# One decoder step on one core: sample bias table, page indices and first weight loads moved to the first two stages, and sample scores on column halves

## The reference

```
mod = silu(c) @ w_ada + b_ada                       # shift, scale, gate, twice
h = x * (1 + sc1) + sh1
mix = mixer(h @ w_in)                               # attention
x = layer_norm(ALPHA * x + (1 + g1) * (mix @ w_o))
h = x * (1 + sc2) + sh2
x = layer_norm(ALPHA * x + (1 + g2) * hier_moe(h))  # 16 experts, 2 per token
```

## Time and profile before

| | us |
|---|---|
| median of 3 runs | 3181.93 (3181.4 to 3189.69) |
| profiled execution, own time | 3175.63 |
| its span, first to last instruction | 3174.2 |
| PE busy in the span | 2614.7 (82%) |
| DVE, ACT, POOL busy | 651.6, 507.9, 443.4 |
| mean granted TensorE clock | 0.90 |

### The profile page before, as it was taken

One profiled execution on the slowest core, in us unless ns is written; L12 is line 12 of the kernel. 1 busy time (PEld: TensorE's weight loads), 2 busy tenths in 40 slices (PEclk: granted clock), 3 DMA queues, 4 the chain that ended last, 5 costly groups with the idle time before them and its releaser, 6 DMA issues. The chain is left out here.

```text
span 3174.2 us, 39101 instructions
## 1 busy us (share of the span) xinstructions
PE 2614.7 (82%) x15984; PEld 1359.7 (43%) x15984; DVE 651.6 (21%) x1761; ACT 507.9 (16%) x1222; POOL 443.4 (14%) x670
## 2 busy tenths in 40 slices
PE   5699999999999945666768637998999599999970
PEld 2244444444444523454545434554445244444430
DVE  0100000000000001122223245773243211111108
ACT  1000000000000002222322325662000011111111
POOL 1000100000001112323110113551000100100110
PEclk9799999999999957788878868999999699999995
DMA  7765847749558324635378424456555389988735
GB/s 316 284 221 204 320 184 261 274 150 345 213 212 310 126 81 188 240 135 225 121 224 308 150 72 148 145 189 215 182 203 177 143 312 338 367 311 276 266 113 185
DMA packets 222305, 693.11 MB, mean 218 GB/s; under 512 B 27360, under 2 KB 41920, under 8 KB 194763
## 3 DMA queue, kind: packets, MB, share of 16 engines
q1 hardware_dynamic: 180212, 478.77, 42.4%
q0 software_dynamic: 38896, 201.85, 17.3%
q10 hardware_dynamic: 3024, 9.96, 0.8%
HBM read 664.01 MB, written 166.88 MB: 262 GB/s over the span
## 5 line engine op out<-in xcount | busy, mean ns | idle before, releaser
L426 PE MATMUL bank<-ring,xt 128*128 128x512 f32 (+1 forms) x2048 | 852.2, 577 | 19.7 <-PEq L436 11.6
L426 PEld LDWEIGHTS bank<-ring,xt 128*128 128x128 f32 x2048 | 378.7, 191 | 484.0 <-issue 472.2
L2812 PE MATMUL bank<-ring,hsT 128*128 128x512 f32 x768 | 339.7, 596 | 0.8 <-DVE hsT L2871 0.8
L2130 PE MATMUL bank<-ring,xt 128*128 128x512 f32 x512 | 224.8, 599 | 8.4 <-DMA ring<-in_w_o 8.4
L2812 PEld LDWEIGHTS bank<-ring,hsT 128*128 128x128 f32 x768 | 144.9, 191 | 174.8 <-issue 173.6
L460 DVE TENSOR_TENSOR mod<-bank,mod 128x512 f32 x4 | 2.8, 691 | 970.7 <-PE bank L215 970.7
L452 ACT ACTIVATE proj_stage<-bank 128x512 f32<-128x512 f32 (+2 forms) x80 | 41.1, 514 | 958.9 <-PE bank L426 938.7
L2831 PE MATMUL bank<-wd,hidT 128*128 128x512 f32 x384 | 171.2, 599 | 11.4 <-ACT hidT L2858 11.4
L2130 PEld LDWEIGHTS bank<-ring,xt 128*128 128x128 f32 x512 | 97.5, 192 | 128.6 <-issue 128.6
L472 POOL DMA_DIRECT2D proj<-proj_stage x64 | 35.3, 551 | 825.9 <-ACT proj_stage L452 825.9
L215 PE MATMUL bank<-ring,ct 128*32 128x512 f32 x768 | 106.5, 694 | 33.6 <-DMA ring<-in_w_ada 33.2
(11 more groups left out here) (466 smaller groups left out, 2613.3 us busy)
## 6 DMA issues: line engine op xcount, KB each, us to landing
ring<-in_w_ada SPq DMA_DIRECT2D x48, 2048.0 KB, 16.3
ring<-in_w_gate_up SPq DMA_DIRECT2D x48, 2048.0 KB, 9.8
ring<-in_w_in SPq DMA_DIRECT2D x30, 2048.0 KB, 9.1
out<-in_cache_dil POOLq DMA_DIRECT2D x7, 8176.0 KB, 41.9
wd<-in_w_down SPq DMA_DIRECT2D x24, 2048.0 KB, 9.4
ring<-in_w_o SPq DMA_DIRECT2D x16, 2048.0 KB, 9.6
ring<-in_cache_dil SPq DMA_DIRECT2D x16, 1024.0 KB, 13.9
rows<-in_cache_dil SPq DMA_DIRECT2D x16, 1024.0 KB, 11.6
```

What stands on the lines that cost most here:

```text
L426: mm = pe.matmul(R.banks[t][0:n, 0:width], R.xt[:, 8 * s + k, t0:t0 + n], R.ring[:, s, k, 0:width], start=(s == 0 and k == 0), stop=(s == ...
L2130: mm = pe.matmul(u_bank[u % 5][:, :], R.xt[:, k, t * P:(t + 1) * P], R.ring[:, sl + k // 8, k % 8, :], start=(k == 0), stop=(k == KT - 1))
L2812: last = pe.matmul(gu_bank[:, :], hsT[j % 2][:, 8 * half + k, :], R.ring[:, 2 * (j % 2) + half, k, :], start=(half == 0 and k == 0), stop= ...
```

## The change

- The bias row stage loads `rowid` and the page table, makes `idx_all`, spreads `tbl` into `tblq`, and issues the first four `load_ada` of the next stage.
- The modulation stage makes `bias_s`: POOL loads the one-hot table in 6 chunks of up to 512 columns into a buffer of two; TensorE multiplies chunk c before product 3 + 2c; VectorE copies it out. The first addition of `b_ada` comes behind the copy of chunk 2.
- The sample stage has one block. POOL begins to gather after two small memsets on VectorE. The loads of queries, keys, small tables and gates come ahead of SP's loop, the transposes ahead of TensorE's first compression, the sigmoid of the gates ahead of ScalarE's first copy, and the block-diagonal queries ahead of VectorE's loop. The staging of the queries moves from `ring` to `e`.
- Score products use 64 columns of the array each, and write to their own half of the output partitions.

```diff
@@ phase_ada
         @block.sync
-            for n in range(8 * NB):
-                load_ada(R, eng, w_ada, n // 8, n % 8, n % 4, n - 3 if n >= 4 else None)
+            for n in range(4, 8 * NB):
+                load_ada(R, eng, w_ada, n // 8, n % 8, n % 4, n - 3)
         @block.gpsimd
+            def one_hots(c):
+                eng.dma_start(ohs[:, c % 2, :, 0:bw[c]], I["oh_smp"].rearrange("p (q c) -> p q c", q=DS)[:, :, 512 * c:512 * c + bw[c]]).then_inc(oh_in[c % 2], 16)
...
                 eng.dma_start(xn[0:n, t % 2, :], src).then_inc(x_in[t % 2], 16)
+                if t == 1:
+                    one_hots(0)
+                    one_hots(1)
+                if t >= 2:
+                    eng.wait_ge(bias_ps, t - 1)
+                    one_hots(t)
+            eng.wait_ge(bias_ps, NC - 2)
+            one_hots(NC - 1)
             eng.wait_ge(ct_zero, 2)
...
         @block.tensor
+            def sample_bias(c):
+                pe.wait_ge(oh_in[c % 2], 16 * (c // 2) + 16)
+                if c >= 2:
+                    pe.wait_ge(bias_done, c - 1)
+                for q in range(DS):
+                    last = pe.matmul(ps_b[c % 2][:, 0:bw[c]], tblq[:, q, :], ohs[:, c % 2, q, 0:bw[c]], start=(q == 0), stop=(q == DS - 1))
+                last.then_inc(bias_ps, 1)
             for n in range(8 * NB):
+                if 3 <= n < 3 + 2 * NC and n % 2:
+                    sample_bias((n - 3) // 2)
...
         @block.vector
+            for c in range(NC):
+                dve.wait_ge(bias_ps, c + 1)
+                dve.tensor_copy(R.bias_s[:, 512 * c:512 * c + bw[c]], ps_b[c % 2][:, 0:bw[c]]).then_inc(bias_done, 1)
+                if c == 2:
+                    dve.wait_ge(b_in, 64)
+                    modulation(0)
+            for b in range(1, NB):
+                modulation(b)
@@ phase_bias_rows
         @block.sync
+            eng.dma_start(rowid[:, :], I["rowid"]).then_inc(idx_in, 16)
+            eng.dma_start(pt_i[:, :], I["page_table"].rearrange("b g -> (b g)").rearrange("(a c) -> a c", a=1).to_broadcast([P, P])).then_inc(idx_in, 16)
+            for n in range(4):
+                load_ada(R, eng, w_ada, n // 8, n % 8, n, None)
@@ phase_nsa_sample
-        with nc.Block() as block:
...
         @block.gpsimd
                 eng.sem_inc(s["pg_free"], CR + 1)
+                eng.wait_ge(s["set"], 2)
                 with eng.Fori(0, DB // 2) as it:
...
         @block.tensor
-                        last = pe.matmul(s_b[k % 2][:, 0:width(k)], qbd[:, pr, :], kts[k % 2][:, pr, 0:width(k)], start=(pr == 0), stop=(pr == 1))
+                        last = pe.matmul(s_b[k % 2][64 * pr:64 * pr + 64, 0:width(k)], qbd[:, pr, 64 * pr:64 * pr + 64], kts[k % 2][:, pr, 0:width(k)],
+                                         start=True, stop=True)
...
+                pe.wait_ge(s["in"], 16 * 8)
...
                 compress(0, 0)
...
         @block.scalar
+                act.wait_ge(s["gate_in"], 16 * NH)
+                act.activation(gates, gates, ACT.Sigmoid).then_inc(s["setup_act"], 1)
                 kc_evac(0, 0)
+                act.wait_ge(s["setup"], 4 * G + 1)
...
         @block.vector
+                dve.memset(small[:, 128:152], 0.0).then_inc(s["set"], 1)
+                dve.memset(neg1, -1.0).then_inc(s["set"], 1)
+                dve.memset(qbd_all[:, :, :, :], 0.0)
+                dve.drain()
+                dve.wait_ge(s["ps"], 1)
...
+                dve.wait_ge(s["setup_act"], 1)
                 with dve.Fori(0, DB // 2) as it:
```

More of the change, by code:

```diff
@@ L230, in phase_ada @@
         xn = R.sb("xn", [P, 2, D], ctx=ctx)
+        ohs = R.sb("ohs", [33, 2, 4, 512], ctx=ctx)
+        oh_in = [R.sem(f"oh_in{s}", ctx) for s in range(2)]
+        bias_ps = R.sem("bias_ps", ctx)
+        bias_done = R.sem("bias_done", ctx)
         c_in = R.sem("c_in", ctx)
@@ L317, in _, with modulation @@
         def _(dve):
+            def modulation(b):
+                dve.wait_ge(R.ring_used, 8 * b + 8)
+                dve.tensor_tensor(mod[:, b, :], ps_mod[b][:, :], mod[:, b, :], ALU.add).then_inc(mod_done, 1)
             dve.memset(ct[:, :, :], 0.0).then_inc(ct_zero, 1)
@@ L540, in _ @@
                 dve.tensor_copy(dst, src).then_inc(rows_done, 1)
+            dve.wait_ge(tbl_in, 16)
+            dve.wait_ge(tblq_set, 1)
+            for q in range(DS):
+                dst = tblq[:, q, :].rearrange("p (k r) -> p k r", k=KV)[:, :, 0:24].rearrange("p k (g q) -> p k g q", q=DS)[:, :, :, q]
+                dve.tensor_copy(dst, tbl[:, 0:NH].rearrange("p (k g) -> p k g", k=KV))
+            dve.wait_ge(idx_in, 32)
+            dve.tensor_scalar(R.idx_all[:, :], pt_i[:, :], float(PAGE), rowid[:, 0:1], ALU.mult, ALU.add)
             dve.wait_ge(ws_set, 1)
@@ L1335, in phase_nsa_sample @@
         idx = R.sb("idx", [P, 2, 16], U32, ctx=ctx)
[L1337 to L1343, removed]
+        sq = e[0:NS, 0:1536]
+        s = {n: R.sem("ns_" + n, ctx) for n in ("in", "gate_in", "set", "ps", "setup", "setup_act", "o_out",
              "idx_slot", "pg_free", "win_in0", "win_in1", "comp", "kc_ready", "qbd_ready", "kt_ps", "kt_ready", "s_ps", "s_read",
@@ L1520, in new_scores @@
                         for pr in range(2):
-                            last = pe.matmul(sm[:, NS * kind:NS * kind + NS], qbd[:, pr, :], knt[:, kind, pr, :], start=(pr == 0), stop=(pr == 1))
+                            last = pe.matmul(sm[64 * pr:64 * pr + 64, NS * kind:NS * kind + NS], qbd[:, pr, 64 * pr:64 * pr + 64], knt[:, kind, pr, :],
+                                             start=True, stop=True)
                     last.then_inc(s["small_ps"], 1)
@@ L1599, in after @@
                     last.then_inc(s["small_ps"], 1)
+                pe.wait_ge(s["in"], 16 * 8)
+                for pr in range(2):
+                    for g in range(G):
+                        src = sq[:, (pr * G + g) * P:(pr * G + g + 1) * P]
+                        last = pe.transpose(B[6][:, (pr * G + g) * NS:(pr * G + g + 1) * NS], src, R.ident[0:NS, 0:NS])
+                last.then_inc(s["ps"], 1)
+                for kind in range(2):
+                    for pr in range(2):
+                        last = pe.transpose(B[7][:, (2 * kind + pr) * NS:(2 * kind + pr + 1) * NS],
+                                            skv[:, 2 + 2 * kind, pr * P:(pr + 1) * P], R.ident[0:NS, 0:NS])
+                last.then_inc(s["ps"], 1)
                 for n in ("kc_ready", "kt_ready", "pt_ready", "exps", "qbd_ready"):
```

131 lines of the change are left out of this document (44 added, 87 removed).

## The result

| | before | after |
|---|---|---|
| median (runs), us | 3184.8 (4) | 3107.24 (4) |
| lowest to highest | 3181.4 to 3189.69 | 3097.53 to 3110.31 |
| profiled execution, span | 3174.2 | 3108.8 |
| mean granted clock | 0.90 | 0.90 |

The ratio after to before is 0.975, 95% interval 0.9723 to 0.9777: a gain of 71 to 88 us, 77.6 by the medians. I had said 3100 us.

A forecast was written before the change was run, and what follows sets the result against it. TensorE bounds the projection stage, full DMA engines the modulation stage, work order and page gathers the sample loop. Gains of 5+56+20 = 81 us from 3175.63 gave 3094.6, plus 6.3 for the median 3101, stated as 3100; range 3083 to 3125.

The forecast's parts named there:

- Early loads: Modulation stage: first four weight loads issued at 4.05 us instead of 18.64, no longer behind the barrier; 14.6 us earlier.
- The gap: Modulation stage: DMA engines idle for 2.5 us because load 4 waits for product 0, which waits for conditioning rows.
- One-hots: Modulation stage: the 1.45 MB table in 33 rows passes while DMA is full; costs 6 us, ends 3.5 and 14.5.
- Part A: Modulation stage: weights start earlier, less the costs of the work added there; 5 us gained, ends +11 and -10.
- TensorE's added products and the copy behind modulation(0): Modulation stage: 24 more products cost 1 us (0 to 10); chunk 3's copy behind b_ada costs nothing, uncovered up to 5.
- Rival 1: Modulation stage loses its head start: one-hots cost 14.5 us or TensorE falls behind; -10 not +5, 3115 us; chance 0.12.
- Part B: Sample stage setup: moved out or hidden under the gather, which starts 57.8 us earlier; gain 56 us, ends 45 and 58.
- Rival 2: Sample stage setup does not hide: loads or instructions arrive only after both gathers (+44 us); time 3112; chance 0.12.
- Part C: Sample loop: score products on column halves run side by side, 0.8 us less each warm; gain 20 us, ends 6 and 28.
- rival 3: Sample loop: the halves do not run side by side; gain 61 us in all, time 3120; chance 0.07.
- The stall in the middle batches: Sample loop: six batches wait on instruction fetch behind gather packets, so faster products ahead of it are worth nothing.
- rival 4: Sample loop: less work keeps TensorE's clock low; gain lost at 0.61, at worst 3244 us; chance 0.03.

The follow-up runs named there:

- run 3: Changed kernel with its first four weight loads issued behind the barrier again, in the modulation stage; 3118.3 us, ratio 0.9788.
- run 4: Changed kernel with four of the six one-hot chunks loaded in their first 16 columns only; 3101.14 us, ratio 0.9743.
- run 6: Changed kernel where POOL also waits for the 24 gate transfers before its first page gather; 3114.81 us, ratio 0.9786.
- runs 7 to 11: Changed kernel with page gathers spread by POOL additions or limited in flight, 3082.79 to 3104.48 us; with drains as well, 3524.17 us.
- run 2: Changed kernel with full-width score products again, so without the column halves; 3126.74 us, ratio 0.9823.
- step_2: Changed kernel with two one-column POOL additions and no drain ahead of each page gather; 3082.79 us, ratio 0.9688.

## Why the prediction was right

Steps in the order of the prediction, sizes from all profiles that share the code.

- **Early loads.** Issue at 4.10 (4.05 forecast), worth 14.5 us. The gap cost 1 us instead of 2.5. Right.
- **One-hots: the step that failed, in size.** I took 6 us of 3.5 to 14.5 from the 262 GB/s of 33-row tables. It is 11 us (run 3), of which 8.7 go by bytes if the rate of run 4 holds for the whole table. Those tables passed alone; beside the weights a MB in 33 rows takes the time of 2.5 MB. Why it is more, no run shows. The 217 GB/s at full share in the earlier trace rows was the warning, and I put it at the end of the range.
- **Part A in sum.** 5 us forecast; product 15 at 118.4 to 119.1 in eight profiles with this stage as it is in the changed kernel, against 121.06 and 120.83, 2.1 us. The sample stage starts 1.7 us earlier (1117.4 against 1119.1 by the means), but 1120.22 and 1117.88 in the two profiles without the change lie further apart than that; what is sure is product 15. The ends that I gave (+11 and -10) leave out the gap of 2.5 us that the sum has.
- **TensorE's added products and the copy behind modulation(0)** cost nothing that shows as a wait of the weight products: the copies of chunks 3 and 4 ran at 100.37, behind b_ada as foreseen, and chunk 5's product at 106.19 did not wait for them. The denser work did not hold the clock up, though: 0.79 from 18.60 to 122.40, where it was 0.82. Rival 1, on the same cause, had the direction right and overstated it (-10 us): the one-hots came to 11, not 14.5, and TensorE kept up.
- **Part B.** 56 us forecast; from stage start to compressed keys 109.8 and 110.2 us without it, 55.1 to 56.8 in five profiles with it, by the means a gain of 54.1. The gather starts at 1.5 us instead of 1.1, the moved loads cost it 3 us instead of 2, all else is hidden (run 6). Rival 2 fell with it.
- **Part C.** 20 us forecast, 17.0 measured. Batches 0 and 7 gave 7.3 (8 forecast), the six middle ones 1.6 each, 9.7 (15 less the 3 for the clock, so 12). Warm and cold lengths were as read, so rival 3 fell. But the sum charges nothing for a change of width, and each costs 0.1 us (the rows under the result), so a warm product between full-width rows saves 0.6 us and not 0.8. The earlier trace rows do not show such a change to be free: the second group does start before the modelled end of the first, by 0.07 us, but rows of one width overlap by 0.16. A batch has seven such changes between rows that follow each other, so up to 0.7 us; how much of the 3 us that part C fell short this is, no run separates.
- **The stall in the middle batches.** I read it as instruction fetch, and that is not shown: the earlier trace rows name only something outside the engines, and the packets do not fit (runs 7 to 11). The part of the sum that rests on it, that products ahead of the stall are worth nothing, needs only the stall itself.
- **Clock.** 0.78 in the loop, far from the 0.61 of rival 4; run 2 shows that the halves lower it. TensorE's busy time in the loop is 230.3 us and not 210, mostly since more of it runs at the lower level: rival 4's 177 us of full-speed work are 224 us at 0.79.
- **Sum.** 1.7+54.1+17.0 = 72.8 us by stretches, inside the timed 71 to 88; the forecast was 81. The mechanisms of the sum held but for the change of width, which it has at nothing; the terms were some 8 us too kind in all (3.3 in A, 1.9 in B, 3.0 in C), and the medians of this comparison (77.6) happened to fall nearer to the forecast than the stretches do: that the time came within 7 us is in part luck. Nor do the first three rivals add up to 3125, as I wrote: singly they stand at 3112 to 3120, all at once they would give 3147, so the range held one of them at a time.

## What to carry to other kernels

A setup that only prepares constants belongs under an earlier stage, but the stage whose DMA was full here paid for small-row tables by more than their bytes: 2.5 times for 33 rows (6 us a MB against 2.4), and some 7 times for 9 (17 us a MB). Price them at the worst row in the same stage, not at the best row of the same shape. When engines stand on nothing that the profile names while a gather runs at a share of 1.0, slow the gather's issue until the stall goes (here at a share of 0.89 to 0.93) and weigh that against the wait for pages which takes its place. Before packing small products side by side, count the changes of width that they bring in.

## What was not expected of the hardware

- 0.29 MB in 9 rows cost 4.9 us of a full DMA stage (17 us a MB), with a share of 1.03 before and 1.02 after: the share doesn't show the loss, only GB/s do (218 and 335).
- Behind an indirect gather, a drain on POOL held it for 3.3 to 5.0 us; an addition of one column with a semaphore takes 0.2 us.
- With TensorE at the upper clock a change between 128 and 64 columns costs 0.1 us, and side-by-side halves still take 1.01 us from start to start of the next row instead of 1.72.
- The first compression, while the next batch is gathered, crawls: in the changed kernel the timeline has single products 1.4 to 2.8 us apart from 1154.93 to 1163.34. With gathers every 1.59 us, in step_2, it has 5 to 24 in a row there.
